# All softmax blocks of a sliding-window attention turned by VectorE and DRAM instead of half of them by TensorE

## The reference

```python
h = rms_norm(x, pre_norm)
q, k, v, gate_a, u_b, v_b, gate_b, mg_a, mg_b = jnp.split(h @ w_in, offsets, axis=-1)
# A: 16 query heads, 2 key/value heads, head dim 64, window 128, blocks of 128 queries
scores = einsum('bnqhgd,bnkhd->bnhgqk', qb, kb) * 64 ** -0.5   # 128 queries x 256 keys a block
scores = where(mask, scores + bias, NEG_INF)                   # bias: T5 buckets of the distance
m = maximum(max(scores), sink); p = exp(scores - m)
probs = p / (sum(p) + exp(sink - m))
o_a = einsum('bnhgqk,bnkhd->bnqhgd', probs, vb)
y_a = (o_a * silu(gate_a)) @ w_branch_a
# B: chunked spatial gating, chunks of 128
mixed = einsum('gts,bnsgd->bntgd', tril(w_s), layer_norm(gelu(v_b))) + b_s
y_b = (gelu(u_b) * mixed * silu(gate_b)) @ w_branch_b
merged = sigmoid(mg_a) * y_a + sigmoid(mg_b) * y_b
x + rms_norm(merged @ w_out, post_norm)
```

## Time and profile before

| | before |
|---|---|
| runs | 908.57, 909.6, 911.26 us |
| profiled execution | 908.92 us |
| its span | 907.2 us |
| TensorE busy | 894.8 us (99%) |
| VectorE busy | 671.5 us (74%) |
| ScalarE busy | 500.9 us (55%) |
| GpSimd busy | 498.2 us (55%) |
| the DMA queue that SyncE feeds | 126.66 MB, 45.7% of 16 engines' span |

### The profile page before, as it was taken

One profiled execution on the slowest core, in us unless ns is written; L12 is line 12 of the kernel. 1 busy time (PEld: TensorE's weight loads), 2 busy tenths in 40 slices (PEclk: granted clock), 3 DMA queues, 4 the chain that ended last, 5 costly groups with the idle time before them and its releaser, 6 DMA issues.

```text
span 907.2 us, 12749 instructions
## 1 busy us (share of the span) xinstructions
PE 894.8 (99%) x4268; PEld 746.9 (82%) x4268; DVE 671.5 (74%) x1167; ACT 500.9 (55%) x982; POOL 498.2 (55%) x395
## 2 busy tenths in 40 slices
PE   9999999999999999999999989999999999999997
PEld 7888788888888888888888868888888888888886
DVE  6766695576666666757576669688689878989968
ACT  6554254775767676666767664334443434534563
POOL 3564235777787777787869636445542252043236
PEclk9999999999999999999999999999999999999999
DMA  8788764433434346534343443533289550435004
GB/s 311 194 201 241 240 209 105 136 104 86 134 88 127 95 117 163 150 105 117 102 116 103 116 146 105 186 117 123 62 292 334 185 209 1 139 114 211 1 1 185
DMA packets 170512, 130.90 MB, mean 144 GB/s; under 512 B 58552, under 2 KB 139472, under 8 KB 170320
## 3 DMA queue, kind: packets, MB, share of 16 engines
q1 hardware_dynamic: 168208, 126.66, 45.7%
q10 hardware_dynamic: 2240, 3.43, 1.2%
HBM read 93.87 MB, written 39.35 MB: 147 GB/s over the span
## 4 chain that ended last, share of the span: by engine, by line
PE 84%; DVE 5%; ACT 4%; issue 3%; SPq 2%; DMA 1%; POOL 0%; DVEq 0%; POOLq 0%; ACTq 0%
PE acc L1019 42%; PE acc L1200 11%; PE ps_m L1200 7%; PE ps_t L1200 7%; PE acc L872 7%; PE ps_t L1036 2%; PE acc L962 2%; PE ps_m L1067 2%; SPq L506 1%; ACT prob L1570 1%; DVE neg_s L2137 1%; DVE pt_pack L2151 1%; ACT prob L1578 1%; DVE ps_t L2134 1%; PE ps_t L1046 1%
## 5 line engine op out<-in xcount | busy, mean ns | idle before, releaser
L1019 PE MATMUL acc<-mv,w_hi 128*128 128x512 f32 x1344 | 353.8, 392 | 0.0
L1019 PEld LDWEIGHTS acc<-mv,w_hi 128*128 128x128 f32 x1344 | 244.8, 188 | 44.9
L1019 PE MATMUL acc<-mv,w_lo 128*128 128x512 f32 x672 | 182.0, 393 | 0.0
L1813 POOL TENSOR_TENSOR w_lo<-sums,w_hi 128x1024 fp32r<-128x1024 f32 x48 | 118.0, 2460 | 73.1 <-ACT w_hi L1366 48.9
L1019 PEld LDWEIGHTS acc<-mv,w_lo 128*128 128x128 f32 x672 | 126.7, 189 | 28.6
L1813 POOL TENSOR_TENSOR w_lo<-raw,w_hi 128x1024 fp32r<-128x1024 f32 (+1 forms) x48 | 95.2, 1984 | 40.1 <-ACT w_hi L1359 32.6
L1570 ACT ACTIVATE prob<-neg_s,neg_max 128x129 f32<-128x129 f32 x128 | 50.5, 396 | 89.7 <-DVE neg_max L2137 89.6
L1200 PE MATMUL acc<-right,left 128*128 128x512 f32 x432 | 98.7, 389 | 0.0
L1200 PEld LDWEIGHTS acc<-right,left 128*128 128x128 f32 x432 | 81.0, 188 | 17.2 <-DVE left L2203 0.4
L2151 DVE TENSOR_TENSOR pt_pack<-turned_in,pt_pack 128x256 fp32r<-128x256 f32 x32 | 43.6, 1362 | 42.5 <-ACT pt_pack L1588 42.5
L1857 POOL TENSOR_SCALAR_AFFINE_SELECT pt_prev<-pt_pack 128x512 fp32r<-128x512 f32 x64 | 40.8, 638 | 58.6 <-DVE pt_pack L2127 39.8
(11 more groups left out here) (286 smaller groups left out, 1688.0 us busy)
## 6 DMA issues: line engine op xcount, KB each, us to landing
raw<-in_w_in SPq DMA_DIRECT2D x56, 512.0 KB, 4.5
ht_d<-sums SPq DMA_DIRECT2D x8, 512.0 KB, 4.9
mix_d<-mix_b SPq DMA_DIRECT2D x8, 512.0 KB, 4.0
prob_d<-prob SPq DMA_DIRECT2D x32, 128.0 KB, 2.2
turned_in<-prob_d SPq DMA_DIRECT2D x128, 32.0 KB, 2.2
ga_d<-gate SPq DMA_DIRECT2D x16, 256.0 KB, 4.1
tb<-tb_d SPq DMA_DIRECT2D x4, 1024.0 KB, 5.1
ub<-mix_d SPq DMA_DIRECT2D x7, 512.0 KB, 3.4
```

Source lines behind the costliest of these rows:

```text
L1019: ins = nc.tensor.matmul(bank, (w_lo if y == 2 else w_hi)[:, left + k * P:left + (k + 1) * P], right[:, (OPW if y == 1 else 0) + k * HALF: ...
L1813: nc.gpsimd.tensor_tensor(w_lo[:, c], src, w_hi[:, c].bitcast(f32), ALU.subtract).then_inc(wlo_ok, 1)
```

## The change

All 64 blocks go the way over VectorE and DRAM. TensorE's transposes are gone. ScalarE copies the returned block into PSUM (`ps_q`, the place of `ps_p`), and VectorE makes hi and lo from there for every block (`cast`). `turned_in` has two halves, `prob` rotates over three buffers for all blocks, `neg_s` has one buffer. On VectorE the transposes stand before the scores of the same step; on ScalarE the copy stands before `norm` and `exps`. Even blocks: away at 3j+2, back at 3j+3, copied and cast at 3j+5. Odd blocks: away at 3j+3, back at 3j+4, copied and cast at 3j+6. Both are selected at 3j+6, and both their values are taken at 3j+7. The bias is spread for one head pair at a time, the first on ScalarE's queue at the old place, the others on SyncE at step 7 of the pair before. The first `u_mix`, and the first `u_mul` with it, come two steps later (s = 5).

```diff
@@ buffers @@
-                turned_in = sb("turned_in", [P, 256], f32, s1)
+                turned_in = sb("turned_in", [P, 512], f32, s1)
-                neg_s = sb("neg_s", [P, 4 * SINK_W], f32, s1)
+                neg_s = sb("neg_s", [P, 2 * SINK_W], f32, s1)
-            buf = prob[2] if s % 2 else prob[s // 2 % 2]
-            return buf[:, h * SINK_W:h * SINK_W + width]
+            return prob[s % 3][:, h * SINK_W:h * SINK_W + width]
@@ SyncE @@
             def attend(p, k):
-                for blk in even_at(k, 2):
-                    prob_away(4 * p + blk // 2)
-                for blk in even_at(k, 3):
-                    prob_back(4 * p + blk // 2)
+                for blk in even_at(k, 2) + odd_at(k, 3):
+                    prob_away(8 * p + blk)
+                for blk in even_at(k, 3) + odd_at(k, 4):
+                    prob_back(8 * p + blk)
+                if k == 7 and p + 1 < HEAD_PAIRS:
+                    sp.dma_start(*skew(p + 1)).then_inc(bias_out, 16)
@@ TensorE @@
-                for blk in odd_at(k, 5) + even_at(k, 7):
+                for blk in even_at(k, 7) + odd_at(k, 7):
                     values(p, blk)
-                for blk in odd_at(k, 3):
-                    transpose_p(p, blk)
                 for blk in blocks_at(k, 0):
                     scores(p, blk)
@@ ScalarE @@
+            def turned_copy(p, blk):
+                s = 8 * p + blk
+                act.wait_ge(prob_in[s % 2], 64 * (s // 2 + 1))
+                if s:
+                    act.wait_ge(ptl_ok, s)
+                nc.scalar.activation(ps_q, turned(s), ACT.Copy).then_inc(turn_in, 1)
             def attend(p, k):
+                for blk in even_at(k, 5) + odd_at(k, 6):
+                    turned_copy(p, blk)
                 for blk in blocks_at(k, 1):
                     norm(p, blk)
                 for blk in blocks_at(k, 0):
                     exps(p, blk)
-                for blk in even_at(k, 5):
-                    turned_hi(p, blk)
@@ GpSimd @@
-                for blk in even_at(k, 6) + odd_at(k, 3):
-                    pool.wait_ge(ptl_ok, place(p, blk))
+                for blk in even_at(k, 6) + odd_at(k, 6):
+                    pool.wait_ge(ptl_ok, 8 * p + blk + 1)
@@ VectorE @@
+            def cast(p, blk, src):
+                pack = pt_pack[blk % 2]
+                own.link(nc.vector.tensor_copy(pack[:, 0:256], src))
+                nc.vector.tensor_tensor(pack[:, 256:512], src, pack[:, 0:256].bitcast(f32), ALU.subtract).then_inc(ptl_ok, 1)
+                for blk in even_at(k, 5) + odd_at(k, 6):
+                    dve.wait_ge(turn_in, 8 * p + blk + 1)
+                    cast(p, blk, ps_q)
+                for blk in blocks_at(k, 1):
+                    dve.wait_ge(prob_ok, 8 * p + blk + 1)
+                    for h in range(2):
+                        w = prob_w(8 * p + blk, h, P)
+                        ins = nc.vector.transpose(w, w)
+                    ins.then_inc(turn_ok, 1)
                 for blk in blocks_at(k, 0):
...
-                for blk in even_at(k, 1):
-                    dve.wait_ge(prob_ok, 8 * p + blk + 1)
...
@@ first mix @@
-                    if kind(n) == "U" and n < PAIRS - 1:
+                    if FIRST_U < n < PAIRS - 1:
                         u_mix(n)
+                if s == 5 and n == FIRST_U:
+                    u_mix(n)
+                    u_mul(n, 0)
```

More of the change, by code:

```diff
@@ L40 @@
 POOL_FRONT = 5
+POOL_SINKS = POOL_FRONT + HEAD_PAIRS
 Q_COL = 0
@@ L299, in build @@
             sem("scores_ok"), sem("scores_used"), sem("exp_ok"), sem("inv_ok"), sem("prob_ok"))
[L300 to L302 removed]
+        prob_out = [sem(f"prob_out{b}") for b in range(2)]
+        prob_in = [sem(f"prob_in{b}") for b in range(2)]
+        turn_ok, turn_in, ptl_ok, pt_ok, values_ok = (
+            sem("turn_ok"), sem("turn_in"), sem("ptl_ok"), sem("pt_ok"), sem("values_ok"))
         otmp_ok, oadd_ok, og_ok = sem("otmp_ok"), sem("oadd_ok"), sem("og_ok")
@@ L489, in odd_at, with turned @@
             return [2 * j + 1 for j in range(4) if 3 * j + lag == k]
-        def place(p, blk):
-            return 8 * p + (blk ^ 1) + 1
+        def turned(s):
+            return turned_in[:, s % 2 * 256:(s % 2 + 1) * 256]
         @block.sync
@@ L639, in load_bias @@
             def load_bias(p):
-                if p == 0:
-                    sp.wait_ge(bias_out, 32)
-                else:
+                sp.wait_ge(bias_out, 32 + 16 * p)
+                if p:
                     sp.wait_ge(scores_used, 8 * p)
@@ L1038, in scores @@
                 ins.then_inc(scores_ok, 1)
-            def transpose_p(p, blk):
-                s = 8 * p + blk
-                pe.wait_ge(prob_ok, s + 1)
-                if s > 1:
-                    pe.wait_ge(ptl_ok, place(p, blk) - 2)
-                for h in range(2):
-                    ins = nc.tensor.transpose(ps_p[:, h * P:(h + 1) * P], prob_w(s, h, P), ident[:, :])
-                ins.then_inc(pt_done, 1)
             def values(p, blk):
-                pe.wait_ge(pt_ok, place(p, blk))
-                if p == 0 and blk == 1:
+                pe.wait_ge(pt_ok, 8 * p + blk + 1)
+                if p == 0 and blk == 0:
                     pe.wait_ge(vlo_ok, 2)
-                if p == HEAD_PAIRS // 2 and blk == 1:
+                if p == HEAD_PAIRS // 2 and blk == 0:
                     pe.wait_ge(v_in, 16)
-                if p == HEAD_PAIRS // 2 and blk == 5:
+                if p == HEAD_PAIRS // 2 and blk == 4:
                     pe.wait_ge(v_out, 32)
                 g = 4 * p + blk // 2
-                if blk % 2 and g >= 2:
+                if blk % 2 == 0 and g >= 2:
                     pe.wait_ge(oadd_ok, g - 1)
@@ L1563, in exps @@
                 if blk == 0:
-                    act.wait_ge(sink_ok, p + 1)
-                if s % 2 and s > 1:
-                    act.wait_ge(pt_done, s // 2)
-                if s % 2 == 0 and s >= 4:
-                    act.wait_ge(prob_out, 16 * (s // 2 - 1))
+                    act.wait_ge(pool_own, POOL_FRONT + p + 1)
+                if s >= 3:
+                    act.wait_ge(prob_out[(s - 3) % 2], 16 * ((s - 3) // 2 + 1))
                 for h in range(2):
-                    ins = nc.scalar.activation(prob_w(s, h, SINK_W), neg_w(blk, h), ACT.Exp, scale=-1.0, bias=neg_max[:, head(blk, h)],
+                    ins = nc.scalar.activation(prob_w(s, h, SINK_W), neg_w(h), ACT.Exp, scale=-1.0, bias=neg_max[:, head(blk, h)],
                                                accum_out=row_sum[:, head(blk, h)])
@@ L2137, in attend @@
                         ins = nc.vector.tensor_tensor_reduce(
-                            out=neg_w(blk, h)[:, 0:P], in0=ps_s[:, h * 256 + P:(h + 1) * 256], in1=bias_t[:, bias:bias + P],
+                            out=neg_w(h)[:, 0:P], in0=ps_s[:, h * 256 + P:(h + 1) * 256], in1=bias_t[:, bias:bias + P],
                             scale=-HEAD_DIM ** -0.5, scalar=sink_b[:, 2 * p + h:2 * p + h + 1], op0=ALU.add, op1=ALU.min,
```

89 lines of the change are left out of this document (33 added, 56 removed).

## The result

The changed kernel took 968.3 us (median of four runs, 966.8 to 971.0), the kernel before 910.4 us in the same session: a ratio of 1.064 with a 95% interval of 1.061 to 1.066. The forecast was 938 us with a range up to 950. The direction was right; the loss is 58 us and not 28. The profiled execution of the changed kernel was its slowest, 971.0 us.

The account below looks back on a forecast made before the run. TensorE's own work was taken as the bound (busy 894.8 of 907.2 us). Sum: 908.9 - 7.0 (transposes) + 40 (late values) - 3.2 (first mix) - 1.1 (bias) = 937.6, so 938 us, range 908 to 950.

Parts of the forecast that it names:

- the bias: Spreading by head pairs: 1.1 us less in the front; the other seven spreads, on SyncE at step 7, hidden.
- Rival D: Twice the returns; a landing some 3 us later delays the next pair's exponentials, 1 to 2 us a pair: 945-955 us, chance 0.06.
- Transposes off TensorE: 32 odd blocks lose two transposes each on TensorE, 0.22 us a block: 7.0 us less, all on the path.
- the inversion: VectorE's transposes ahead of the same step's scores delay ScalarE's exponentials and copies: 1.67 + 0.7 + 1.15 us a pair.
- Steps 7, 10 and 13: TensorE waits for odd blocks' values: 3.3 us at steps 7 and 10, 1.7 at 13; 40 us in eight pairs.
- Step 13's own terms: Copy of block 5 follows that of block 3 by 11.5 us, TensorE needs 9.7: late by 1.7 us a pair.
- the distance alone: Lower bound without inserted transposes, only copies nearer their values: 0.4 and 0.6 us late, 8 us in all.
- The wait of ScalarE ahead of odd exponentials: VectorE transposes the previous block before taking the scores, so ScalarE goes on 1.67 us later.
- First mix: Read two steps later: 5.6 us less, 2.4 us new wait at step 16 from VectorE's gating work; net 3.2 less.
- the 0.8 us beside it: TensorE's wait at one score product, expected to go with the first mix's 4.8 us.
- Front: Wait of 1.1 us there goes with only one pair's 384 KB of bias ahead (bounds 0 and 1.5).
- SyncE: Four issues per return, now for 64 blocks, hold it some 30 of a pair's 47 us; costed at nothing.

Follow-up runs that it names:

- wide form: Changed kernel, same bias spreads issued by SyncE at step 7, but with the 128 copies outermost instead of the two heads: 942.7 us, ratio 1.037.
- spread_once: Changed kernel, but the bias of all heads spread by one transfer on ScalarE's queue in the first stretch, as before the change: 943.4 us, ratio 1.037.

## Why the prediction was wrong

The step that failed is one sentence on the bias: "The other seven go through SyncE at step 7, four steps ahead of their use, hidden there." The use of a spread was looked at and the queue behind it wasn't, though the prediction names SyncE's queue elsewhere. The price is 25.6 us with the rest of the change as it is (968.3 against 942.7 us for the wide form at the same place). The only duration of a spread that the prediction had was that of the earlier trace rows, where 3072 KB take 15.8 us. By bytes alone 384 KB would be 2 us; the narrow form took some ten. Rival D had a return three microseconds late, but by the doubled returns, and at 0.06.

- **Transposes off TensorE, 7.0 us less.** Right. With the inversion and the spreads out, a pair takes 46.53 us with a wait of 0.52 in it, so 46.0 without; the forecast had 45.9.
- **Steps 7, 10 and 13, 5.0 us a pair, 40 us.** Right in mechanism and size, once the spreads are out: 51.12 us a pair against 45.9 is 5.2 us, and 51 had been forecast. Step 13's own terms add up to 1.8 us a pair and not 1.7, and ScalarE's stretch there (383.27 to 391.68) had idle times of 0.23, 0.43 and 0.83 us, so the reason given for the 40 us, a run without a gap, held for the stretch before it only. That the size came out so close is in part luck. The three waits stand at these steps. The inversion was put at 3.5 of the 5.0 us and is 4.6 of 5.2 (51.12 - 46.53); the distance alone was put at 1.0 and leaves some 0.6.
- **The wait of ScalarE ahead of odd exponentials, 1.7 us.** 1.56 to 1.57 us at blocks 3 and 5 of the second pair, right.
- **First mix, 3.2 us net less.** Wrong in the term for what takes the old wait's place. It was bounded at 3.4 us and is a wait of 4.87 us, and its reason was another: not VectorE's gating work ahead of the casts but block 5's return behind the `bmat` load. This too is an in-order queue passed by unread. Of the saving, the 4.8 us for the wait and its slow stretch were right, 4.9 us where it stands alone; the 0.8 us beside it was no part of it and stayed. That the net came out near zero instead of at 3.2 us is the new wait.
- **Front, 1.1 us less.** The first pair starts 1.5 us earlier (160.88 against 162.42), at the upper bound.
- **SyncE, nothing.** Right for the returns themselves: with wide spreads a pair takes what the sum without any SyncE term gives.
- **Not in the sum: the clock.** The forecast's waits were short, and behind the 0.89 us at step 13 no slow stretch follows. Behind six of the seven longer ones that came instead the next stretch ran 0.9 to 2.3 us longer.

The sum with the measured terms in place: 908.9 - 7.0 + 41.5 (5.2 us in eight pairs) - 1.5 + 25.6 = 967.5, beside the 968.3 measured, with the mix near zero. This is close in part because errors cancel: the first pair loses less than 5.2 us (it takes 48.6 us with wide spreads).

The profiled executions of the changed kernel and of *spread_once* lie 29 us apart (971.0 and 941.7). Of these the longer waits at step 13 of seven pairs make 12 (18.3 us in place of seven times 0.89), and the slow stretches behind them 8.

What stays open: over all pairs, which part of the 25 us is the store waiting for its shares on the two engines and which the long issue (2.18 us) was not told apart. In the second pair the issue is 1.3 of the 3.1 us that the other queue saves; why the queue matters beyond that, no run shows. The mechanism inside the DMA engines is inferred from the share of busy engines and the experiment on the order of dimensions.

## What to carry to other kernels

When a transfer moves, read what is queued behind it, and how it is cut up, not only when its own data are wanted: a small copy with a small outermost dimension held a store of 128 KB behind it for ten microseconds here. On an in-order engine, a step that waits for a neighbour's fresh result belongs behind the step whose result that neighbour needs next; 0.5 us of work in the wrong order cost 4.6 us a pair. Price the parts of a bundle apart: here two small edits gained some 7 us (910.1 to 903.0) and the large one, repaired, nothing, and two losses hid a part of one another (60 us together, 46 as the sum of each undone alone).

## What was not expected of the hardware

- While 384 KB with the two heads outermost were on the way, the 16 DMA engines had a busy share of 0.13 to 0.15 and moved 37 to 44 GB/s (from 242 to 244 and from 248 to 252 us); the same bytes with 128 outermost landed in 4.4 us.
- The store issued right behind the narrow transfer took 2.18 us to issue (4.35 us in another pair and kernel) where 0.56 is usual, and landed after up to 10.5 us, in the kernel before with narrow spreads up to 12.3 us, where 2.2 to 2.4 is the median.
- After a gap of 2.55 us in TensorE's work the clock was granted at 0.50 for over two microseconds, which cost 1.0 us; behind a gap of 2.54 us in the first pair it stayed at 1.00, and behind the gaps of 0.89 us the same stretch took its usual 2.76 us.
